# A fused two-block transformer on one Trainium2 core: gated tiles' products two steps at a time at every second attention unit

## What is computed

```python
def _even_mixer(x, w_in, w_out, ...):
    gq, gk, gv, glr, gr, nq, kc, vc, ks, vs, kw, vw, ng = jnp.split(x @ w_in, offsets, axis=-1)
    o_a = _gla(gq, gk, gv, glr, gr, ...)       # 4 heads of 128; ends in  o * silu(r)
    o_b = _nsa(nq, kc, vc, ks, vs, kw, vw, ...)  # 8 heads of 64
    return jnp.concatenate([o_a, o_b], axis=-1) @ w_out
```

## Time and profile before

| what | value |
|---|---|
| median of 3 runs | 2076.81 us (2076.64 to 2078.31) |
| the profiled execution's own time | 2076.55 us |
| its span, first to last instruction | 2074.8 us |
| TensorE matmuls busy (PE) | 99% of the span |
| TensorE weight loads busy (PEld) | 82% |
| DVE / ACT / POOL busy | 48% / 34% / 17% |
| DMA, mean | 101 GB/s |
| mean granted TensorE clock | 0.998 |
| the attention's loop | 171.5 to 265.3 us of the span |

### The profile page before, as it was taken

How to read it: one execution, slowest core, us unless ns; L and a number is a source line. 1 busy time by engine, 2 the same in 40 slices (tenths; PEclk the granted TensorE clock), 3 DMA queues, 4 the chain that set the end, 5 groups by cost and what they waited for, 6 DMA issues and landing times. The chain is left out here.

```text
span 2074.8 us, 27643 instructions
## 1 busy us (share of the span) xinstructions
PE 2046.2 (99%) x11274; PEld 1704.2 (82%) x11274; DVE 1001.7 (48%) x1388; ACT 704.8 (34%) x1013; POOL 349.1 (17%) x207
## 2 busy tenths in 40 slices
PE   9999999999999999999999999999999999999998
PEld 7876688888887999888888888888877788888886
DVE  5346758538254435625736334632433564332345
ACT  6365644222123432314313212534333243122212
POOL 2000005858820001000586000000000100000000
PEclk9999999999999999999999999999999999999999
DMA  7211024544533232232454232232121232322331
GB/s 227 75 50 40 22 94 140 183 131 163 174 95 107 82 92 82 81 112 82 152 179 128 99 102 85 79 102 73 61 62 61 82 102 82 112 95 88 101 101 61
DMA packets 138986, 209.46 MB, mean 101 GB/s; under 512 B 5306, under 2 KB 114040, under 8 KB 138872
## 3 DMA queue, kind: packets, MB, share of 16 engines
q1 hardware_dynamic: 129904, 180.89, 27.1%
q0 software_dynamic: 6912, 25.17, 3.7%
q10 hardware_dynamic: 2056, 1.76, 0.3%
HBM read 205.70 MB, written 2.10 MB: 100 GB/s over the span
## 5 line engine op out<-in xcount | busy, mean ns | idle before, releaser
L1283 DVE TENSOR_TENSOR w_lo<-w_raw,w_hi 128x2048 fp32r<-128x2048 f32 x151 | 351.2, 2326 | 550.5 <-ACT w_hi L685 550.2
L1941 PE MATMUL ps<-x_hi,w_hi 128*128 128x512 f32 x1248 | 495.8, 397 | 2.6 <-DVE w_lo L1283 1.9
L1943 PE MATMUL ps<-x_hi,w_lo 128*128 128x512 f32 x1248 | 486.9, 390 | 0.0
L1942 PE MATMUL ps<-x_lo,w_hi 128*128 128x512 f32 x1248 | 486.9, 390 | 0.0
L685 ACT ACTIVATE w_hi<-w_raw 128x2048 fp32r<-128x2048 f32 x152 | 290.7, 1912 | 504.1 <-PE ps L1943 397.3
L1941 PEld LDWEIGHTS ps<-x_hi,w_hi 128*128 128x128 f32 x1248 | 235.0, 188 | 59.8 <-issue 11.3
L1943 PEld LDWEIGHTS ps<-x_hi,w_lo 128*128 128x128 f32 x1248 | 234.5, 188 | 49.4
L1942 PEld LDWEIGHTS ps<-x_lo,w_hi 128*128 128x128 f32 x1248 | 234.8, 188 | 45.9 <-issue 0.5
L1941 PE MATMUL ps<-w_hi,h_hi 128*128 128x512 f32 x688 | 269.2, 391 | 1.3 <-DVE col_bias L1661 1.3
L1942 PE MATMUL ps<-w_lo,h_hi 128*128 128x512 f32 x688 | 268.7, 391 | 0.0
L1943 PE MATMUL ps<-w_hi,h_lo 128*128 128x512 f32 x688 | 268.6, 390 | 0.0
(11 more groups left out here) (363 smaller groups left out, 2757.2 us busy)
## 6 DMA issues: line engine op xcount, KB each, us to landing
w_raw<-in_ffn_w SPq DMA_DIRECT2D x64, 1024.0 KB, 5.4
ada_w<-in_w_ada POOLq DMA_DIRECT2D x48, 512.0 KB, 4.2
w_raw<-in_w_ffn_in SPq DMA_DIRECT2D x22, 1024.0 KB, 5.1
w_raw<-in_w_in SPq DMA_DIRECT2D x20, 1024.0 KB, 5.3
w_raw<-in_o_w_in SPq DMA_DIRECT2D x16, 1024.0 KB, 5.7
w_raw<-in_w_ffn_out SPq DMA_DIRECT2D x11, 1024.0 KB, 4.9
w_raw<-in_e_w_in SPq DMA_DIRECT2D x9, 1024.0 KB, 5.2
w_raw<-in_o_w_out SPq DMA_DIRECT2D x8, 1024.0 KB, 4.8
```

The costliest lines, as they stand in the source:

```text
L1283: nc.vector.tensor_tensor(w_lo[:, slot, :], w_raw[:, slot, :], w_hi[:, slot, :].bitcast(F32), ALU.subtract).then_inc(w_lo_ready, 1)
L1941: nc.tensor.matmul(dst, a_hi, b_hi, start=start, stop=False)
L1942: nc.tensor.matmul(dst, a_hi, b_lo, start=False, stop=False)
L1943: return nc.tensor.matmul(dst, a_lo, b_hi, start=False, stop=stop_)
```

## The change

`r_during` lists the steps of each iteration. Before, a gate tile that starts at unit `at` has one step in each of the 8 iterations `at` to `at + 7`. Now it has two steps in each of the iterations `at`, `at + 2`, `at + 4`, `at + 6` and none in those between. The starts in `r_first` (2, 12 and 22) stay.

```diff
         def r_during(u):
 
-            return [(x, u - at) for x, at in r_first.items() if at <= u < at + DK]
+            return [(x, u - at + step) for x, at in r_first.items() if at <= u < at + DK and (u - at) % 2 == 0
+                        for step in range(2)]
 
         def r_finished(u):
 
             return [x for x, k in r_during(u) if k == DK - 1]
```

## The result

The changed kernel takes 2086.53 us, the median of 6 runs (2084.93 to 2088.17), against 2077.23 for the kernel before (6 runs). The ratio is 1.0044, with a 95% interval of 1.0031 to 1.0057: slower by some 9 us, more than twice the +4.1 of the forecast and beyond its range. The profiled execution took 2087.30 us.

The account below looks back on a forecast made before the run. TensorE, busy 99% of the span, was taken as the bound. Chain waits +4.81, step prices +0.18, vanished stalls -1.59 and small waits +0.7 gave +4.1 us: 2080.9 us against the median 2076.81, range 2078.3 to 2084.4.

Parts of the forecast that it names:

- Price of a step, and the saving by batching: Attention loop on TensorE: single step 0.89 us, second step 0.68; by batching alone 12 x 0.21 = 2.5 us faster.
- The chain over tanh, gate and taking: Products of iterations 10, 20, 30 wait for copy, exponentials, tanh, gate and taking: +1.23, +1.44, +2.14, together +4.81 us.
- The sum at the full clock, +4.1: Whole attention loop: all terms together make the kernel 4.1 us slower, with no term for a clock fall.
- the likeliest case itself: Attention loop: the summed terms hold, centre +4.1 us, granted clock 1.00 throughout; chance 0.55.
- the first rival: New waits of TensorE at iterations 10, 20, 30: clock falls there, 1.6 us each, 2082.5 to 2085.7 us; chance 0.20.
- Rival 2: The 12 even iterations behind emptied odd ones wait 0.25 us more each, or second steps cost 0.89: 2083.4 to 2083.9; chance 0.08.
- term (c): New small waits in even iterations behind an emptied odd one (8, 16, 24, 14, 6): +0.7 us in sum.
- Stalls of 12 and 22 gone: Iterations 12 and 22: stalls of 0.56 and 0.83 us go, as tanh and gate leave the place ahead of the maxima.
- Nothing downstream gives time back: Behind the attention loop: PE is busy to the end, so nothing there gives the lost time back.

Follow-up runs that it names:

- e5: The change with each gate tile starting one iteration later (3, 13, 23), so double steps stand in odd iterations, tanh and gate in 10, 20, 30: 2073.90 us.
- e4: The change with matmuls repeated (scores of units 12 and 22, transposes of unit 30) so TensorE works in its three long waits: 2081.98 us.
- e9: The change with only the transposes of unit 30 repeated, eight times; the waits of iterations 10 and 20 stay idle: 2083.24 us.
- e2: The change with only the last two steps of each gate tile merged (iterations 8, 18, 28), the others single: 2085.51 us.
- e1: The change with ACT's tanh of a completed gate tile ahead of its iteration's copies and exponentials (9, 19, 29): 2074.41 us.
- e3: The change with the first three pairs of steps of each gate tile merged, the last two single, tanh and gate in 10, 20, 30: 2076.65 us.
- e7: The change with DVE's gate alone one iteration later (10, 20, 30), behind the taking of the pair; tanh stays: 2074.72 us.
- e8: The kernel before (single steps) with ACT's tanh ahead of the copies and exponentials of iterations 10, 20 and 30: 2074.78 us.
- e6: e5 with ACT's tanh also ahead of the copies and exponentials of iterations 10, 20 and 30: 2074.83 us.
- e10: e5 with DVE's gate one iteration later (11, 21, 31): 2074.37 us.

## Why the prediction was wrong, step by step

- **Price of a step, and the saving by batching:** right. In the change iteration 2, with its second step, lasts 0.70 longer than before (scores of the next at 179.79 against 179.09), where the prediction had 0.68. Where nothing waits (e5) the loop is 2.25 shorter, where 12 x 0.21 is 2.5.
- **The chain over tanh, gate and taking:** right. The products of iteration 10 were forecast 203.49 - 199.76 = 3.73 us behind the end of iteration 9 and stand 3.71 behind it. Iteration 30 in e4: 3.40, forecast 263.79 - 260.37 = 3.42.
- **The sum at the full clock, +4.1:** right. e4_busy_wait has the same chain at the full clock, and its loop is 4.47 us longer than before; its median is 4.0 over the kernel before at its side.
- **The step that failed is the likeliest case itself: that the clock holds.** The sum has no term for the clock; its fall stood as the first rival with a chance of 0.20 and a price of 1.6 us a fall. It is what happened: 13.6 us at half clock in the profile, worth 5.3 us there and between the times of the change and e4. The price of a short stretch was right (1.5 us), but at iteration 30 a stretch of 10.2 us began, which cost 3.8, where the rival had taken each to last as long as the one of the earlier trace rows. The argument against it, that waits of over a microsecond elsewhere keep the clock, was taken from waits of at most 1.63 us (but for one at the program's very start), and the new ones are longer. The Trainium skill, page TensorE: Matmul & The Clock Gate, section HAM oscillation, has the rule that idle gaps bring the slower clock and that this is paid anew each time. The trace agrees in kind, in gaps shorter than the page's, and not each time: of the eight waits of 2.3 to 2.5 us that were left unfilled, it fell at four (iteration 10 of e9, 20 of e2 and the change, 30 of the change) and held at four (10 of the change and e2, 20 of e9, 30 of e2). The range reached to one fall or two short ones and should have held all three waits.
- **Rival 2, even iterations starved behind an emptied one:** wrong as the cause. e1, e3, e5 and e7 keep most or all double steps and are not slower than before. The small waits that term (c) had at 0.7 us are there: 0.2 each at 8, 16 and 24 and 0.15 at 6 and 14, some 0.9 together.
- **Stalls of 12 and 22 gone:** right in the change. Iterations 12 and 13 together last 5.43 us, against 6.23 before and 5.69 in e8, which has the early tanh and single steps.
- **Nothing downstream gives time back:** right; the +9.3 of the time is the loop's +8.24 and what the half clock does behind it, and the span of that profile holds one more fall than the kernel before's, at 1458 us.

## What to carry to other kernels

When work of the busiest engine is moved, follow what its completion triggers on the other engines, in their written order: here the matmuls moved by one iteration, and what cost was a gate on DVE that came to stand ahead of the one taking that TensorE waits for. Let an instruction that waits for late work stand behind all those on which the bound engine waits, or make its input early; either edit turned a loss of 9 us into a gain, of some 3 us by the medians and 1.6 to 1.7 us in the loop. And price a new wait of TensorE at the full clock and once more with the half clock behind it, since here the second part (5.3 us) was as large as the first (4.5 us).

## What the runs showed of the hardware that was not expected

The clock does not fall behind the same wait in each execution, even where the wait is the same. Far behind the loop, at 1335.9 us in the kernel before and 1332.1 in e1_tanh_first, TensorE waits 1.6 us for DVE, with narrow transposes behind it. Before (the stretch with the wait, and the one behind it):

```profile
1335.80:1339.30 3.50, 1.53 (x12) 1.09 (x11) 2.56 (x5) 1.44 (x3) 0.00 (x0) 1.00 0.00 0
1339.30:1342.70 3.40, 3.40 (x30) 3.40 (x31) 1.60 (x4) 2.79 (x6) 0.00 (x0) 1.00 0.02 5
```

and the same two stretches in e1_tanh_first:

```profile
1332.00:1335.50 3.50, 1.54 (x13) 1.10 (x11) 2.52 (x5) 1.44 (x3) 0.00 (x0) 1.00 0.00 0
1335.50:1338.90 3.40, 3.40 (x17) 3.40 (x17) 1.39 (x4) 2.58 (x6) 0.00 (x0) 0.50 0.02 5
```

In the kernel before the clock stayed at 1.00; in e1 it went to 0.50 behind the wait, and e1 in turn has no fall at 628.9, where the kernel before has one. The runs of a kernel fall into groups: e4_busy_wait has four at 2079.8 to 2080.3, five at 2081.8 to 2082.8 and one at 2086.8. The profiles bear out that one stretch at half clock more or less makes the small steps. Take the loop from the span: 1979.9 to 1980.5 us are left in the five profiles with one such stretch between the loop and the program's last 20 us (before, e1, e5, e7 and e8), and 1981.4 to 1982.6 in the five with two (e2, e3, e6, e9 and e10), 1.7 us more on average. The 0.8 us of loop between e5 on one side and e6 and e10 on the other is hidden in that.

It also qualifies the gains of e1, e7 and e8: their profiles and that of the kernel before have one stretch each, and from span to span they are 2.2, 2.0 and 1.7 us shorter, close to their loops (1.7, 1.6, 1.4), while the kernel before's own profiled execution (2076.55) lies 1.3 to 1.4 us under the medians that they are compared with.

The large step, some 5 us, is in e4's profile the late start shown above; that it is the same in the other runs that lie so far up, as five of the 19 of the kernel before at 2082.4 to 2082.8, was not profiled. What decides in a given execution whether a wait of this size brings the slower clock stays open.
